# Norming the latent rows for the next layer inside the out-projection, and taking six tiles latent-first

## What is computed

```python
h = rmsnorm(x, g_pre) * (1 + scale) + shift      # modulation per layer and stream
y = mixer(h_latent, h_context)                   # ends in  @ w_out
x = x + gate * rmsnorm(y, g_post)

def rmsnorm(x, g):
    xf = x.astype(jnp.float32)
    y = xf * lax.rsqrt(jnp.mean(xf * xf, axis=-1, keepdims=True) + EPS)
    return (y * g.astype(jnp.float32)).astype(x.dtype)
```

## Time and profile before

| | us |
|---|---|
| Median of 3 runs | 2556.64 |
| Lowest, highest | 2554.22, 2557.5 |
| The profiled execution, its own time | 2556.34 |
| Its span | 2554.5 |
| VectorE busy | 932.6 (37%) |
| ScalarE busy | 641.6 (25%) |
| POOL busy | 46.8 (2%) |
| DMA, mean over the span | 222 GB/s |

### The profile page before, as it was taken

The page is one execution under the profiler, slowest core; times in us unless marked ns, Lnnn a source line. Parts: engine busy times, 40 slices in busy tenths (PEclk is TensorE's granted clock), DMA queues, the critical chain, the costliest instruction groups (busy, mean ns, idle before and its releaser), DMA issues. The chain is left out here.

```text
span 2554.5 us, 31840 instructions
## 1 busy us (share of the span) xinstructions
PE 2390.3 (94%) x11948; PEld 1282.4 (50%) x11949; DVE 932.6 (37%) x2135; ACT 641.6 (25%) x1480; POOL 46.8 (2%) x57
## 2 busy tenths in 40 slices
PE   6999999999999988899899779999999999999998
PEld 5545685468645557676786553333233323332332
DVE  2207624042610583527354433233223222322333
ACT  3016623243210353226331321111111111111111
POOL 0000000000100000100001000000000000000000
PEclk8999999999999998999899789999999999999999
DMA  8117931200121002239331048699989998999897
GB/s 298 66 66 268 347 108 58 83 34 34 66 67 66 34 1 99 100 130 327 105 133 66 36 175 350 257 418 417 418 343 418 418 418 349 418 418 418 346 418 307
DMA packets 154254, 568.00 MB, mean 222 GB/s; under 512 B 10832, under 2 KB 12368, under 8 KB 121136
## 3 DMA queue, kind: packets, MB, share of 16 engines
q1 hardware_dynamic: 154160, 566.72, 56.8%
HBM read 565.64 MB, written 1.05 MB: 222 GB/s over the span
## 5 line engine op out<-in xcount | busy, mean ns | idle before, releaser
L2397 PE MATMUL PS<-BIG,PW 128*64 128x512 f32 x2304 | 514.5, 598 | 21.1 <-DMA BIG<-in_w 21.1
L2397 PEld LDWEIGHTS PS<-BIG,PW 128*64 128x64 f32 x2304 | 158.7, 137 | 375.2 <-issue 310.8
L2421 PE MATMUL PS<-BIG,PW 128*64 128x512 f32 x1152 | 255.1, 595 | 8.6 <-ACT PW L2497 8.6
L2556 DVE TENSOR_SCALAR PW<-PS 128x512 f32<-128x512 f32 x36 | 24.9, 692 | 538.0 <-PE PS L2397 538.0
L2494 ACT ACTIVATE PW<-PW 128x512 f32<-128x512 f32 x36 | 22.7, 630 | 772.3 <-DVE PW L2556 772.3
L2421 PEld LDWEIGHTS PS<-BIG,PW 128*64 128x64 f32 x1152 | 79.3, 137 | 161.3 <-issue 144.1
L884 PE MATMUL PS<-HT,BIG 128*128 128x512 f32 (+1 forms) x448 | 155.0, 504 | 0.0
L557 PE MATMUL PS<-HT,BIG 128*128 128x256 f32 x640 | 139.5, 379 | 2.1 <-PEq L666 2.1
L557 PEld LDWEIGHTS PS<-HT,BIG 128*128 128x128 f32 x640 | 121.4, 190 | 19.0 <-issue 1.8
L884 PEld LDWEIGHTS PS<-HT,BIG 128*128 128x128 f32 x448 | 86.3, 193 | 62.9 <-issue 56.9
L1183 PE MATMUL PS<-BIG,HT 128*128 128x512 f32 x256 | 110.0, 592 | 0.0
(11 more groups left out here) (455 smaller groups left out, 3133.4 us busy)
## 6 DMA issues: line engine op xcount, KB each, us to landing
BIG<-in_w SPq DMA_DIRECT2D x384, 1024.0 KB, 16.6
BIG<-in_l_w_ada SPq DMA_DIRECT2D x24, 2048.0 KB, 8.9
BIG<-in_l_w_in SPq DMA_DIRECT2D x20, 2048.0 KB, 7.8
BIG<-in_w_ada SPq DMA_DIRECT2D x12, 2048.0 KB, 8.2
BIG<-in_l_w_out SPq DMA_DIRECT2D x8, 2048.0 KB, 9.3
BIG<-in_w_in SPq DMA_DIRECT2D x7, 2048.0 KB, 9.2
BIG<-in_w_out SPq DMA_DIRECT2D x2, 2048.0 KB, 8.0
BIG<-in_l_w_in SPq DMA_DIRECT2D x1, 1792.0 KB, 12.0
```

Of the source, the lines that this page charges most:

```text
L2397: ins = nc.tensor.matmul(PS[64 * g:64 * g + 64, 4 + half, :], xt[:, c % 4, c // 4, :], W[:, c, half * F + g * 512:half * F + g * 512 + 512 ...
L2421: ins = nc.tensor.matmul(PS[64 * g:64 * g + 64, 7, :], at_[:, k % 4, k // 4, :], W[:, 8 + k // 2, k % 2 * D + g * 512:k % 2 * D + g * 512 ...
```

## The change

The latent rows of layer l + 1 are normalised and modulated at the end of the out-projection Block of layer l: VectorE makes the gain and the eight products behind the second inverse root, ScalarE modulates the eight blocks behind its last tile. For that the latent squares move from behind tile (1, 4) to behind (1, 2), and TensorE's second sum from behind (1, 6) to behind (1, 4). The next layer's first block then begins with the context rows alone (`context_vector`, `context_scalar`), and TensorE waits for no latent block. In layers 1 and 2 six tiles instead of four run latent-first, in banks 0 to 5; in layer 3 it stays at four. In layer 1 the sums of the low-rank squares move from behind z tile 0 to z tile 2, and their roots from z tile 2 to z tile 4.

```diff
+        def norm_gain(dve, l, g_pre, streams, part=0):
+            m = modulation(l)[:, 3 * KT * part:, :]
+            dve_chain.link(dve, nc.vector.scalar_tensor_tensor(GAIN[:, :, 0:streams], m[:, KT:2 * KT, :], 1.0,
+                                                               col(g_pre).unsqueeze(2).to_broadcast([P, KT, streams]), ALU.add, ALU.mult))
+        def norm_rows(dve, tok):
+            for k in range(KT):
+                nc.vector.tensor_tensor(HT[:, k, tok], XT[:, k, tok], RSTD[:, tok], ALU.mult).then_inc(S["normed_ready"].sem, 1)
+        def modulate_rows(act, l, s, tok, nth=0, part=0):
+            for k in range(KT):
+                act.wait_ge(*at("normed_ready", nth * KT + k + 1))
+                nc.scalar.activation(HT[:, k, tok], HT[:, k, tok], ACT.Identity, bias=modulation(l)[:, 3 * KT * part + k, s:s + 1],
+                                     scale=GAIN[:, k, s:s + 1]).then_inc(S["h_ready"].sem, 1)
...
+        def context_vector(dve):
+            inverse(dve, CONTEXT)
+            residual(dve, CONTEXT)
+            inverse(dve, CONTEXT, 1)
+            norm_rows(dve, CONTEXT)
+        def context_scalar(act, l):
+            root(act, PS[:, 6, 0:LAT], CONTEXT)
+            for k in range(KT):
+                act.wait_ge(*at("residual_ready", k + 1))
+                square(act, k, CONTEXT, SQ)
+            root(act, PS[:, 7, 0:LAT], CONTEXT, 1)
+            modulate_rows(act, l, 1, CONTEXT)
@@ first_tiles
-                            pe.wait_ge(*at("h_ready", s * KT + k + 1))
+                            if not pending:
+                                pe.wait_ge(*at("h_ready", s * KT + k + 1))
+                            elif tok is CONTEXT:
+                                pe.wait_ge(*at("h_ready", k + 1))
@@ project_out, tensor
-                        if (s, m) == (1, 6):
+                        if (s, m) == (1, 4):
                             sum_added(pe, LATENT, PS[:, 5, 0:LAT])
@@ project_out, scalar
+                        if (s, m) == (1, 2):
+                            squares()
                         if (s, m) == (1, 4):
-                            squares()
-                        if (s, m) == (1, 6):
                             root(act, PS[:, 5, 0:LAT], LATENT, 1)
+                    if beside:
+                        modulate_rows(act, l + 1, 0, LATENT)
@@ project_out, vector
                     inverse(dve, LATENT, 1)
                     if beside:
+                        norm_gain(dve, l + 1, f"l{l + 1}_g_pre", 2)
+                        norm_rows(dve, LATENT)
                         sum_tiles(1)
@@ latent_layer, tensor (and memory_layer likewise)
-                    first_tiles(pe, True, [(j, 2, done[j]) for j in range(4)], latent_or_context)
+                    first_tiles(pe, True, [(j, 2, done[j]) for j in range(6)], latent_or_context)
...
-                        if kind == "z" and m == 0:
+                        if kind == "z" and m == 2:
                             square_sums()
+                            pe.wait_ge(*at("tile_taken", 6))
                             rope(0)
@@ latent_layer, scalar
-                        if kind == "z" and m == 2:
+                        if kind == "z" and m == 4:
                             for n in range(2):
                                 act.wait_ge(*at("inverse_ready", n + 1))
```

More of the change, by code:

```diff
@@ L397, in norm_vector @@
                                                                col(g_pre).unsqueeze(2).to_broadcast([P, KT, streams]), ALU.add, ALU.mult))
-            for tok in (LATENT, CONTEXT)[:streams]:
[L399 to L404, removed]
@@ L406, in norm_scalar @@
-        def norm_scalar(act, l, streams, pending=False, part=0):
-            if pending:
-                root(act, PS[:, 6, 0:LAT], CONTEXT)
-            for s, tok in enumerate((LATENT, CONTEXT)[:streams]):
[L410 to L418, removed]
+        def norm_rows(dve, tok):
+            for k in range(KT):
+                nc.vector.tensor_tensor(HT[:, k, tok], XT[:, k, tok], RSTD[:, tok], ALU.mult).then_inc(S["normed_ready"].sem, 1)
@@ new lines, in modulate_rows, with norm_vector @@
+        def modulate_rows(act, l, s, tok, nth=0, part=0):
[3 more added lines that the diff above has]
+                                     scale=GAIN[:, k, s:s + 1]).then_inc(S["h_ready"].sem, 1)
+        def norm_vector(dve, l, g_pre, streams, part=0):
+            norm_gain(dve, l, g_pre, streams, part)
+            for tok in (LATENT, CONTEXT)[:streams]:
+                norm_rows(dve, tok)
@@ new lines, in norm_scalar @@
+        def norm_scalar(act, l, streams, part=0):
+            for s, tok in enumerate((LATENT, CONTEXT)[:streams]):
+                modulate_rows(act, l, s, tok, nth=s, part=part)
+        def context_vector(dve):
[10 more added lines that the diff above has]
+            modulate_rows(act, l, 1, CONTEXT)
@@ L437, in norm_passed @@
         def norm_passed(streams, pending=False):
-            S["normed_ready"].passed(KT * streams)
-            S["h_ready"].passed(KT * streams)
+            S["normed_ready"].passed(KT if pending else KT * streams)
+            S["h_ready"].passed(KT if pending else KT * streams)
             if pending:
@@ L622, in project_out @@
                 S["squares_added"].passed(1)
+                S["normed_ready"].passed(KT)
+                S["h_ready"].passed(KT)
             for n in ("square_sum_ready", "rms_ready"):
@@ L890, in _ @@
                 def _(act):
-                    norm_scalar(act, i, 2, pending)
+                    if pending:
+                        context_scalar(act, i)
+                    else:
+                        norm_scalar(act, i, 2)
                     for j, (kind, m, c, x, tok) in enumerate(tiles):
@@ L899, in _ @@
                 def _(dve):
-                    norm_vector(dve, i, f"l{i}_g_pre", 2, pending)
+                    if pending:
+                        context_vector(dve)
+                    else:
+                        norm_vector(dve, i, f"l{i}_g_pre", 2)
                     for n, j in enumerate(roped):
@@ L985, in latent_or_context @@
                             return nc.tensor.matmul(PS[:, j, t], w[:, k, j * P:(j + 1) * P], HT[:, k, t], start=(k == 0), stop=(k == KT - 1))
+                        if tiles[j][0] == "z":
+                            if k == 0:
+                                ws.wait(pe, tiles[j][2])
+                            return nc.tensor.matmul(PS[:, j, t], ws.view(tiles[j][2])[:, k, (j - 4) * P:(j - 3) * P], HT[:, k, t],
+                                                    start=(k == 0), stop=(k == KT - 1))
                         for half in range(2):
@@ L1165, in latent_or_context @@
                     def latent_or_context(j, k, t):
-                        return nc.tensor.matmul(PS[:, j, t], ws.view(c_in)[:, k, j * P:(j + 1) * P], HT[:, k, t], start=(k == 0),
-                                                stop=(k == KT - 1))
+                        if j == 4 and k == 0:
+                            ws.wait(pe, c_in + 1)
+                        return nc.tensor.matmul(PS[:, j, t], ws.view(c_in + j // 4)[:, k, j % 4 * P:(j % 4 + 1) * P], HT[:, k, t],
+                                                start=(k == 0), stop=(k == KT - 1))
                     ws.wait(pe, c_in)
-                    first_tiles(pe, True, [(j, 2, done[j]) for j in range(4)], latent_or_context)
+                    first_tiles(pe, True, [(j, 2, done[j]) for j in range(6)], latent_or_context)
                     for j, (kind, m, c) in enumerate(tiles):
-                        if j < 4:
+                        if j < 6:
                             continue
@@ L1199, in _ @@
                 def _(act):
[L1200 removed]
+                    context_scalar(act, 2)
                     for j, (kind, m, c) in enumerate(tiles):
                         act.wait_ge(*done[j])
[L1203 removed]
+                        o = PS[:, j if j < 6 else j % 4, :]
                         if kind == "g":
```

15 lines of the change are left out of this document (7 added, 8 removed).

## The result

| | before | changed |
|---|---|---|
| Median of 18 runs each, us | 2556.22 | 2560.62 |
| Lowest, highest | 2553.51, 2558.54 | 2558.12, 2566.88 |
| Profiled execution | 2556.34 | 2559.21 |
| Its span | 2554.5 | 2557.1 |

A forecast was written before the change was run, and what follows sets the result against it. TensorE, busy 94% of the span, was taken to bound the kernel, held at three seams between layers by the preceding block's end and the context chain. +2.9 + 1.2 - 1.7 - 0.4 = +2.0 gave 2558.5, range 2554.0 to 2563.0.

The forecast's parts named there:

- first rival: Seams start at full clock, TensorE waits 2.4, the fourth tile loses 1.7 in layers 1 and 2: 2561.9, chance 0.13.
- Modulations ahead of the barrier: Between layers, ScalarE's eight latent modulations behind its last tile delay the next block's start: +2.66 on each of three seams.
- E: End of TensorE's last out-projection tile of a layer, from which the prediction counts times; 382.34 at the first seam.
- The context chain starts sooner: Behind the next block's start, VectorE's context reciprocal no longer stands behind latent products, so POOL's end comes 1.68 sooner.
- point 5: Low clock at seam starts hides in the wait for POOL; layer 1's fourth tile then runs at full clock: -1.7.
- The wait for latent rows is worth nothing by itself: At the block's start TensorE's 1.05 wait goes, but it only reaches the wait for POOL sooner: no gain.
- Early squares: In the out-projection, squares two tiles sooner make TensorE wait 0.2 to 0.7 for POOL, not 0.17: +0.4, three times.
- The rival of full exclusion: In the out-projection POOL and VectorE run strictly one after the other; POOL group longer than 7: 2564.9, chance 0.10.
- Six tiles, -0.4: Two more latent-first tiles in layers 1 and 2 cover late context rows in layer 2: -0.4; layer 1 nothing.
- the modulations don't hold up the next block: At the seams TensorE and VectorE go on at 2.37 behind the last out-projection tile: 2552.1 or 2550.4, chance 0.07.

## Why the prediction was right, and what it missed

The forecast was 2558.5 with "no change" likeliest and slower next; measured were +4.4 against the +2.0 of the sum (against a median 0.4 below the one it started from). The 2560.62 lies in the range (2554.0 to 2563.0), but 0.1 above the forecast's own spread (2556 to 2560.5), and it is nearer to the first rival's 2561.9 than to 2558.5. So the time alone doesn't decide between these two; the rows do. The loss of 0.19% is just under the 0.2% that the prediction calls "no change", though its interval (0.12% to 0.26%) excludes zero: it was a near thing.

1. **Modulations ahead of the barrier, +2.66 a seam.** Shown twice: the block starts at E + 5.03, and with the same eight instructions between the tiles it starts at E + 1.27 and the kernel is 14 us faster than the changed one by medians (2546.59 and 2560.62; the kernel before, run beside each, differed by 1.4).
2. **The context chain starts sooner, -1.68.** This is the term that was mis-sized. It was -1.15 at the first seam. POOL's end moved from E + 17.63 to E + 19.14, so the seam cost 1.51 instead of 0.98; the second cost 1.28 and the third 1.48. I took the context sum at its 0.67 although my own point 5 expected a low clock at that very instruction; I let the slow start count against TensorE's tiles, where the wait hides it, and not against the chain, which begins with a matmul. Kept busy, TensorE gave the forecast's 13.58. In all the three seams cost 1.3 more than the working's 2.9. (From the root's end to the reciprocal's start are 1.72 by the rows, not 1.68; the working leaves unsaid that a reciprocal starts some 0.04 behind its root, as at 390.95 behind 390.92.)
3. **The wait for latent rows is worth nothing by itself:** so it was. TensorE still stands for POOL, 1.08, 1.25 and 0.96.
4. **Early squares, +0.4 a seam:** +0.33. POOL took 5.88 beside VectorE, between my 5.55 and 6.0. The rival of full exclusion (over 7) is out. What I overlooked is a gain hidden in the same edit. Point 1 saw that VectorE's sums would follow the tiles, but not that the early squares alone bring this about, and that the barrier could then fall at E + 1.27. The changed kernel can't use it, because ScalarE is later.
5. **The clock, -1.7 in layer 1:** right, 3.67 instead of 5.36. The waits of 1.08, 1.25 and 0.96 were longer than the 0.6 of the working (13.58 less 12.94), and two of them longer than its "under 1". At the first seam the chain ended 0.53 later than worked out, and TensorE came 0.14 later.
6. **Six tiles, -0.4:** right in sign, but 0.8 in layer 2 by the pace of the full-clock halves, and 0.4 in layer 1, which the working put at nothing. And that they stand behind the wait and can't cover it is shown: with the sum one tile later the wait is gone.

The sum +2.0 became +4.1 in the profiles: 1.3 from the chain, about 1 from the clock in layer 3, where one execution lost more than another, and small differences for the rest. The 0.3 between these rows and the medians isn't traced. Of the rivals, the one by which the modulations don't hold up the next block is refuted by the row at 389.21. The first rival (full clock at the seams and a slow fourth tile) is refuted for the changed kernel by the slow context sums and the fourth tile's 3.67. What it describes did happen in layer 1 with spread modulations and with TensorE kept busy, behind waits of 2.59 and 2.60, but not in layer 2 of either.

## What to carry to other kernels

Work moved ahead of a barrier must fit into gaps of the engine that does it: behind that engine's last item it held up everybody here, and between two items of the same stage, where ScalarE idled for 2.7, it was free. The change lost 4.4 us with ScalarE's 4 us behind the last tile of three stages, and gained 8 with them between two tiles. When a tile is added to cover a wait, look on which side of the waiting instruction it stands. And where a chain of other engines begins with one short matmul, TensorE's clock at that matmul is part of the chain.

## What was not expected of the hardware

A single 128x256 float32 product behind the barrier took 0.67 behind an idle time of 1.3 to 2.4, and 0.84 to 1.19 behind 5.0; behind busy matmuls with 0.30 of idle it was 0.67 again. An idle stretch of 2.5 to 2.6 in front of layer 1's fourth tile was followed by a slow tile in the kernel before, with spread modulations and with TensorE kept busy (5.36, 5.00, 5.36; granted clock 0.62, 0.50 and 0.54 at its start), and by a tile at full speed in the kernel with the early squares alone (3.67, clock 1.00). In layer 2 the tile behind 2.60 was at full speed both times. No run here shows what decides between the two.

POOL's adds lost little beside VectorE, while VectorE's operations beside POOL take 0.83 to 1.00 instead of 0.42 (and the residual beside the latent adds in the changed kernel): if there is a lock between them, it is VectorE that waits. The Trainium skill, page "SBUF — State Buffer", section "SBUF: two separate sides", has the later of the two block fully. Of POOL the runs show 0.05 an add (5.88 against 5.55 for seven), far less than one VectorE operation of 0.42, so here the measurement decides.
